# Sums over heads and latents with tokens on the partitions, roots in narrow tiles, spread back by TensorE

## The chip, the cores and the metric

The kernel runs on one core of a Trainium2 chip. The metric is device time in microseconds (us), from the first to the last instruction and what lies around them. Three runs of the kernel before took 2337.64, 2347.23 and 2343.11 us, median 2343.11.

The core has TensorE (matmuls; PE in the profile, its weight loads PEld), VectorE (DVE), ScalarE (ACT), GpSimd (POOL) and SyncE (SP). Matmul results go to PSUM banks of 128 partitions by 512 fp32 values; all else lies in SBUF with 128 partitions.

## The reference, cut to what matters

The model is a decoder trunk of two layers on 512 tokens and 1024 channels. Each layer norms x, projects it, runs four mixers (gated DeltaNet, MLA, RWKV-7, sparse attention), gates and sums their outputs, projects, and adds; then comes an MLP. All of it is fp32. Four places in the mixers divide by a root that belongs to a head and a token, and one divides by a root that belongs to a token:

```python
def rms_norm(x, g, eps=NORM_EPS):
    x32 = x.astype(F32)
    y = x32 * lax.rsqrt(jnp.mean(x32 * x32, axis=-1, keepdims=True) + eps)
    return (y * g.astype(F32)).astype(x.dtype)

def l2_normalize(x, eps=1e-6):
    x32 = x.astype(F32)
    return x32 * lax.rsqrt(jnp.sum(x32 * x32, axis=-1, keepdims=True) + eps)

# RWKV-7, 4 heads of 64
kk = l2_normalize(heads(k * k_k.astype(F32)))                    # the "keys"
o = ((o - mean) * lax.rsqrt(var + RWKV_GN_EPS)).reshape(b, s, RWKV_W) * ln_w + ln_b   # output norm
# gated DeltaNet, 4 heads of 64
q = l2_normalize(q.reshape(b, s, GDN_HEADS, GDN_DK))
k = l2_normalize(k.reshape(b, s, GDN_HEADS, GDN_DK))
o = rms_norm(o, norm_g) * jax.nn.silu(z)                         # gated output norm
# MLA, latents of 256 and 128 channels
q = rms_norm(c_q, q_norm_g) @ w_uq
kv = rms_norm(c_kv, kv_norm_g) @ w_ukv
```

## The kernel before, in words

Activations lie with channels on the partitions and the 512 tokens along the free side. A tile of 128 channels holds two heads of 64, one on partitions 0 to 63 and one on 64 to 127.

**The projections.** The weights come in units of 128 output channels. For each unit ScalarE splits off a high part (L1020), GpSimd makes the low part (L412), and TensorE does 24 matmuls of 512 columns (L451, L452, L455) into one bank. A "gate unit" is such a projection for one tile of a branch's gate. `gates` does two of them, `merge_outputs` (L499) then projects the branch's output `yo` for the two tiles, and VectorE multiplies by the sigmoid and adds (L1390 or L1394). `merge` is both.

**A sum over a head.** `block_sums` multiplies a tile of squares by the constant `blocks`, 128x128 with ones where row and column belong to the same head. So every one of 64 partitions gets the head's sum for 512 tokens: the sum comes out already spread, 128x512 per tile. VectorE adds the epsilon while copying the bank to SBUF, takes the reciprocal of the wide tile, ScalarE takes the root of the wide tile, and VectorE multiplies. For the latents the same is done with the constant `ones` (L849, L853). The sums of the outputs for the mean (L1562) and of r, k and r_k for the bonus (L1524) are block sums too, which the change leaves alone.

**The order.** There is no scheduler. Each engine has its own program in one fixed order, and semaphores join them. Banks go round in three pools: `bank_a` (three banks, read by ScalarE), `bank_v` (four, read by VectorE) and `bank_f` (one). The pool's next bank is used only when its last reader is done. The five places in TensorE's order:

- Keys of RWKV: `block_sums` between two of the eight RWKV projections. VectorE takes the reciprocal (L1502) before mixing tile 5, ScalarE the root (L1100) after copying tile 5.
- Output norm of RWKV and q, k of the delta rule: `block_sums` for both stand behind each other, after the last delta projections, then four gate units, then the wait for `r_out` (VectorE's L1588), then four L499 products. VectorE takes three reciprocals around there (L1576, L1592, L1621), the last behind the gate arithmetic (L1605 widens the gates, L1619 masks the decays). From L1605 TensorE makes the cumulated gates (L771, L775, L557). L1633 makes the last operand of the chunks, which TensorE wants at L532 (transposes).
- Gated output norm: `block_sums` before the second projection of the sparse attention. VectorE's L1651 and ScalarE's L1188 follow.
- Latents of MLA: L849 and L853, then two gate units and two L499 products, then the wait for VectorE's scaled latents (L1756), then the projections of L860.

Further lines that the text names: L545 and L546 (pair matrices of chunks), L1332 (their masks), L532 and L663 (transposes), L612, L632 and L636 (the scan over chunks, in halves of 64 rows), L655 and L673 (attention), L1533 and L1542 (decayed keys and the convolution on VectorE), L1685 (first step of the selection of keys).

Of the kernel before, what the change touches and what calls it, by code (L numbers as in the profile page):

```python
# [22 lines left out]
P = 128  # L23
# [4 lines left out]
TT = T // P  # L28
C = 64
# [47 lines left out]


# [78 lines left out]
def build(nc, x_in, pos_in, wstream, par_in, const_in, tabs, x_dram, out):  # L157
    ctx = ExitStack()
    with ctx:
# [26 lines left out]
        att = sb("att", [P, 3, 4])  # L186

# [56 lines left out]
        for name, n in (  # L244
# [4 lines left out]
            ("r_ex", 1), ("r_sq", 1), ("r_l2", 2), ("r_l2r", 1), ("r_l2s", 1), ("r_bsq", 2), ("r_bon", 2), ("r_feat", 4),  # L249
            ("r_tok", 8), ("r_mat", 8), ("r_x1", 2), ("r_ti", 2), ("r_y", 10), ("r_t", 8), ("r_x", 10),  # L250
            ("r_wt", 2), ("r_y1", 2), ("r_u", 2), ("r_ws", NC), ("r_s", NC), ("r_o", NC),
            ("r_mean", 2), ("r_sq2", 1), ("r_gv", 2), ("r_gr", 1), ("r_gs", 1), ("r_out", 1),
            ("g_in", 6), ("g_z", 2), ("g_conv", 6), ("g_sig", 6), ("g_sq", 1), ("g_l2", 4),
            ("g_l2r", 1), ("g_l2s", 1), ("g_qk", 1), ("g_t1", 1), ("g_sp", 1), ("g_t2", 1), ("g_g", 2), ("g_feat", 6), ("g_gc", 1),
# [3 lines left out]
            ("g_sq2", 1), ("g_gv", 2), ("g_gr", 1), ("g_gs", 1), ("g_out", 1),  # L258
# [3 lines left out]
            ("m_in", 2), ("m_sq", 1), ("m_nv", 2), ("m_rec", 1), ("m_rs", 1), ("m_c", 1), ("m_q", 4), ("m_k", 4), ("m_v", 2),  # L262
# [169 lines left out]
        def _(pe):  # L432
# [213 lines left out]

            def attention(l, x, q_of, k_of, v, fill):
# [46 lines left out]
            for l in range(L):  # L694
# [101 lines left out]
                for i in range(10):  # L796
# [49 lines left out]
                b, reader, emptied = banks.next("v", "m_nv")  # L846
# [433 lines left out]
        def _(dve):  # L1280
# [159 lines left out]
            for l in range(L):  # L1440
# [144 lines left out]
                for f in range(2):  # L1585
                    ts(R["o"][:, f, :], R["o"][:, f, :], pr("ln_w", f), pr("ln_b", f), MUL, ADD)
# [317 lines left out]
```

## Time and profile before

| | before |
|---|---|
| median of 3 runs | 2343.11 us |
| the profiled execution | 2340.02 us |
| its span, first to last instruction | 2338.2 us |
| TensorE busy, share of the span | 2164.7 us, 93% |
| VectorE | 1193.5 us, 51% |
| ScalarE | 722.6 us, 31% |
| GpSimd | 735.5 us, 31% |
| mean granted clock of TensorE, 1 is full | 0.963 |

A busy engine has an instruction under way. [...] "L451" is line 451 of the kernel. Where a wait of TensorE is put down to a line of VectorE, that line's instruction was the last that it waited for. A granted clock of 1.00 is 2.4 GHz and 0.50 is 1.2 GHz.

### The profile page before, as it was taken

What the parts mean: (1) busy time and instruction counts of PE and PEld (TensorE: products, weight loads), DVE (VectorE), ACT (ScalarE), POOL (GpSimd) and SP (SyncE); (2) the same over time, 40 slices, a digit from 0 to 9 for tenths busy, and PEclk for the clock granted to TensorE, in tenths of its full rate; (3) what the DMA queues carried; (4) which work ended last, traced back from release to release, by engine and by line L of the source; (5) the groups of instructions that cost most, each with busy time, mean ns of one, the idle gap of its engine ahead of it and who ended that gap; (6) DMA issues with size and microseconds to landing.
All of it is one profiled execution on the core that took longest, in us unless ns stands there. A gap on an engine that the chain in (4) does not pass through costs nothing.

```text
span 2338.2 us, 34564 instructions
## 1 busy us (share of the span) xinstructions
PE 2164.7 (93%) x14516; PEld 1662.2 (71%) x14516; DVE 1193.5 (51%) x1847; ACT 722.6 (31%) x1102; POOL 735.5 (31%) x550
## 2 busy tenths in 40 slices
PE   6988898998999899999989888799899998999997
PEld 4777686765566688888758766777565676888885
DVE  5885765897473321212168675569956523212212
ACT  3421321233342342323233124023243423322322
POOL 1520211321213344444425022033212242444442
PEclk7999998999999899999989999999999998999998
DMA  4310101221211232323322011012112121233231
GB/s 155 108 62 14 55 29 37 81 77 45 94 51 59 72 106 92 99 91 98 94 95 85 24 43 51 21 57 76 60 50 104 34 90 60 94 99 93 96 99 55
DMA packets 52265, 170.02 MB, mean 73 GB/s; under 512 B 5648, under 2 KB 13968, under 8 KB 51600
## 3 DMA queue, kind: packets, MB, share of 16 engines
q1 hardware_dynamic: 50928, 162.75, 21.8%
q0 software_dynamic: 1184, 5.07, 0.6%
q8 instruction: 116, 1.90, 0.4%
q14 instruction: 37, 0.30, 0.0%
HBM read 160.45 MB, written 7.34 MB: 72 GB/s over the span
## 4 chain that ended last, share of the span: by engine, by line
PE 76%; DVE 20%; ACT 2%; issue 2%; DMA 1%; SPq 0%; DVEq 0%; ACTq 0%
PE bank_a L451 11%; PE bank_a L452 11%; PE bank_a L455 11%; PE bank_v L455 6%; PE bank_v L451 6%; PE bank_v L452 6%; PE bank_v L557 5%; PE bank_v L499 3%; DVE arena L1697 2%; DVE m L1695 2%; DVE arena L1296 2%; PE bank_v L673 2%; PE bank_v L471 2%; DVE s_z L1373 1%; PE bank_v L655 1%
## 5 line engine op out<-in xcount | busy, mean ns | idle before, releaser
L412 POOL TENSOR_TENSOR w_lo<-ring,w_hi 128x512 fp32r<-128x512 f32 x536 | 729.1, 1382 | 1427.5 <-ACT w_hi L1020 1427.4
L451 PE MATMUL bank_a<-h_hi,w_hi 128*128 128x512 f32 x1440 | 591.4, 411 | 31.8 <-DVE h_lo L1320 29.0
L452 PE MATMUL bank_a<-h_lo,w_hi 128*128 128x512 f32 x1440 | 569.0, 395 | 0.0
L1020 ACT ACTIVATE w_hi<-ring 128x1024 fp32r<-128x1024 f32 x268 | 282.1, 1053 | 354.2 <-DVE arena L1806 273.1
L451 PEld LDWEIGHTS bank_a<-h_hi,w_hi 128*128 128x128 f32 x1440 | 274.0, 190 | 122.7 <-issue 45.1
L455 PE MATMUL bank_a<-h_hi,w_lo 128*128 128x512 f32 x1440 | 358.1, 391 | 0.0
L452 PEld LDWEIGHTS bank_a<-h_lo,w_hi 128*128 128x128 f32 x1440 | 275.3, 191 | 62.9 <-issue 9.1
L455 PEld LDWEIGHTS bank_a<-h_hi,w_lo 128*128 128x128 f32 x1440 | 272.1, 189 | 57.6 <-POOL w_lo L412 0.6
L451 PE MATMUL bank_v<-parts,w_hi 128*128 128x512 f32 x640 | 254.4, 398 | 1.4 <-DVE parts L1783 1.4
L452 PE MATMUL bank_v<-parts,w_hi 128*128 128x512 f32 x640 | 253.4, 396 | 0.0
L1806 DVE TENSOR_TENSOR arena<-arena,bank_v 128x512 f32<-128x512 f32 x64 | 44.1, 689 | 306.2 <-PE bank_v L455 306.2
L1797 DVE TENSOR_TENSOR arena<-arena 128x512 f32<-128x512 f32 x64 | 44.3, 692 | 263.6 <-ACT arena L1261 263.6
L455 PE MATMUL bank_v<-parts,w_lo 128*128 128x512 f32 x640 | 162.2, 395 | 0.0
L451 PEld LDWEIGHTS bank_v<-parts,w_hi 128*128 128x128 f32 x640 | 120.3, 188 | 32.7 <-DVE parts L1783 4.0
L452 PEld LDWEIGHTS bank_v<-parts,w_hi 128*128 128x128 f32 x640 | 120.1, 188 | 29.5 <-issue 0.5
L455 PEld LDWEIGHTS bank_v<-parts,w_lo 128*128 128x128 f32 x640 | 120.2, 188 | 29.1
L557 PE MATMUL bank_v<-arena 64*64 64x64 f32 x3712 | 113.6, 221 | 3.8 <-DVE arena L1345 3.8
L557 PEld LDWEIGHTS bank_v<-arena 64*64 64x64 f32 x3712 | 112.7, 137 | 4.5 <-DVE arena L1345 4.2
L499 PE MATMUL bank_v<-yo,out_ring 128*128 128x512 f32 x256 | 114.0, 592 | 0.0
L1296 DVE TENSOR_TENSOR arena<-arena 128x512 f32<-128x512 f32 (+5 forms) x80 | 96.0, 1200 | 18.1 <-ACT arena L1074 15.5
L1261 ACT ACTIVATE arena<-bank_a 128x512 f32<-128x512 f32 x64 | 38.3, 598 | 210.3 <-PE bank_a L455 210.3
L990 ACT ACTIVATE sg<-bank_a 128x512 f32<-128x512 f32 x56 | 33.4, 596 | 217.9 <-PE bank_a L455 108.9
(270 smaller groups left out, 2469.4 us busy)
## 6 DMA issues: line engine op xcount, KB each, us to landing
ring<-in_w SPq DMA_DIRECT2D x268, 512.0 KB, 3.5
out_ring<-in_w SPq DMA_DIRECT2D x64, 128.0 KB, 3.5
x_dram<-arena SPq DMA_DIRECT2D x2, 2048.0 KB, 8.9
arena<-x_dram SPq DMA_DIRECT2D x2, 2048.0 KB, 7.9
arena<-in_x SPq DMA_DIRECT2D x2, 1024.0 KB, 8.4
arena<-tabs POOLq DMA_DIRECT2D x4, 512.0 KB, 3.9
out_x<-arena SPq DMA_DIRECT2D x2, 1024.0 KB, 4.4
par<-in_par POOLq DMA_DIRECT2D x2, 937.0 KB, 7.0
```

The lines of the kernel that those rows point to most:

```text
L412: ins = nc.gpsimd.tensor_tensor(w_lo[:, g % SPLIT, ks, :], raw, w_hi[:, g % SPLIT, ks, :].bitcast(F32), ALU.subtract)
L451: mm(b[:], w_hi[:, s, k, :], hi[:, k, :], start=k == 0, stop=False)
L452: mm(b[:], w_hi[:, s, k, :], lo[:, k, :], start=False, stop=False)
L455: ins = mm(b[:], w_lo[:, s, k, :], hi[:, k, :], start=False, stop=k == KT - 1)
L471: ins = mm(b[:], cst("ones"), squares[n % 2][:, k, :], start=k == 0, stop=k == KT - 1)
L499: ins = mm(b[:], out_ring[:, n % OUT_RING, k, :], yo[:, slot, k, :], start=k == 0, stop=k == 1)
L557: ins = mm(b[quarter(p_), k * C:(k + 1) * C], lhs[quarter(p_), m, :], rhs(m, p_), start=True, stop=True)
L673: ins = mm(b[rows, 0:P], v[:, k, h * C:(h + 1) * C], V_pt(x)[:, j % 2, k, :], start=k == 0, stop=k == qt)
L1020: act_fn(w_hi[:, g % SPLIT, :, :], ring[:, g % RING, :, :], ACT.Copy).then_inc(S["split_hi"], 1)
L1296: link(v.tensor_tensor(out_, a, b, op))
L1695: link(v.max(m8[:], src))
L1697: link(v.match_replace(wk, m8[:], src, -3e38))
```

## The change

The sums are made with tokens on the partitions. `head_sums` takes the tile of squares as the weights, 128 tokens at a time, and moves two columns (one for each head). So a tile of 128 channels by 512 tokens gives 8 columns in one bank; all tiles of a call go into that bank. `head_recip` reads 16 or 32 columns, scales, adds the epsilon and takes the reciprocal, in a small tile `roots`. `head_sqrt` takes the root of the same columns on ScalarE. `spread_roots` takes one column, repeated 64 times, as the weights and moves the identity: that gives a head's root on 64 partitions for 128 tokens. VectorE then reads that bank as an operand of the product, which it used to read from SBUF. For the latents the sums move one column of ones, and the spread has 128 repeated columns.

In TensorE's order the spreads stand: for the keys after one more RWKV projection; for RWKV's output norm between the two pairs of gate units; for q and k after the cumulated gates (L557); for the gated norm after the next projection; for the latents between the gate units and the L499 products, with a wait for VectorE's three products behind these.

```diff
+        roots = sb("roots", [P, 5, 32])
...
+            def head_sums(l, need, k, src, tiles):
+                pe.wait_ge(S[need], at(l, need, k))
+                b, reader, emptied = banks.next("v", "h_sum")
+                pe.wait_ge(reader, emptied)
+                heads = cst("blocks").rearrange("p (x c) -> p x c", c=C)[:, :, 0]
+                for i in range(tiles):
+                    for t in range(TT):
+                        at_ = (i * TT + t) * 2
+                        ins = mm(b[:, at_:at_ + 2], src[:, i, t * P:(t + 1) * P], heads, start=True, stop=True)
+                ins.then_inc(v_full, 1)
+
+            def spread_roots(l, step, tiles):
+                pe.wait_ge(S["h_rt"], at(l, "h_rt", step + 1))
+                for i in range(tiles):
+                    b, reader, emptied = banks.next("v", "h_bc")
+                    pe.wait_ge(reader, emptied)
+                    for t in range(TT):
+                        at_ = (i * TT + t) * 2
+                        for hp in range(2):
+                            ins = mm(b[quarter(hp), t * P:(t + 1) * P], roots[:, step, at_ + hp:at_ + hp + 1].to_broadcast([P, C]),
+                                     cst("ident"), start=True, stop=True)
+                    ins.then_inc(v_full, 1)
...
-                block_sums(l, "r_sq", 1, R["tmp"], 2, "r_l2")
+                head_sums(l, "r_sq", 1, R["tmp"], 2)
                 pe.wait_ge(S["r_act"], at(l, "r_act", 2))
                 low_rank(pr("g2"), R["rm"][:, 7, :])
-                project_rw(3)
+                project_rw(1)
+                spread_roots(l, ROOT_KK, 2)
+                project_rw(2)
...
-                block_sums(l, "r_sq2", 1, R["sq"], 2, "r_gv")
-                block_sums(l, "g_sq", 1, G["sq"], 4, "g_l2")
+                head_sums(l, "r_sq2", 1, R["sq"], 2)
+                head_sums(l, "g_sq", 1, G["sq"], 4)
                 numbers = gates(l, 2, 0)
+                spread_roots(l, ROOT_R, 2)
                 more = gates(l, 2, 1)
                 pe.wait_ge(S["r_out"], at(l, "r_out", 1))
...
                 for half in range(2):
                     chunk_products("v", "g_row", half, ...)
+                spread_roots(l, ROOT_QK, 4)
                 merge(l, 2, 0, 2)
...
                     if i == 1:
-                        block_sums(l, "g_sq2", 1, G["sq2"], 2, "g_gv")
+                        head_sums(l, "g_sq2", 1, G["sq2"], 2)
                     feat_group(("ds", i), l, h_hi, h_lo, "a", "d_in" if i < 8 else "d_vf")
+                    if i == 1:
+                        spread_roots(l, ROOT_G, 2)
...
-                for k in range(2):
-                    ins = mm(b[:], cst("ones"), Mv["sq"][:, k, :], start=k == 0, stop=k == 1)
+                one = cst("ones")[:, 0:1]
+                for t in range(TT):
+                    tokens = slice(t * P, (t + 1) * P)
+                    mm(b[:, t:t + 1], Mv["sq"][:, 0, tokens], one, start=True, stop=False)
+                    mm(b[:, t:t + 1], Mv["sq"][:, 1, tokens], one, start=False, stop=True)
+                for t in range(TT):
+                    tokens = slice(t * P, (t + 1) * P)
+                    ins = mm(b[:, TT + t:TT + t + 1], Mv["sq"][:, 2, tokens], one, start=True, stop=True)
                 ins.then_inc(v_full, 1)
-                mm(b[:], cst("ones"), Mv["sq"][:, 2, :], start=True, stop=True).then_inc(v_full, 1)
-                merge(l, 3, 0, 2)
-                pe.wait_ge(S["m_c"], at(l, "m_c", 1))
+                numbers = gates(l, 3, 2)
+                pe.wait_ge(S["h_rt"], at(l, "h_rt", ROOT_M + 1))
+                for i in range(2):
+                    b, reader, emptied = banks.next("v", "h_bc")
+                    pe.wait_ge(reader, emptied)
+                    for t in range(TT):
+                        ins = mm(b[:, t * P:(t + 1) * P], roots[:, ROOT_M, i * TT + t:i * TT + t + 1].to_broadcast([P, P]),
+                                 cst("ident"), start=True, stop=True)
+                    ins.then_inc(v_full, 1)
+                merge_outputs(0, numbers)
+                pe.wait_ge(S["h_bc"], at(l, "h_bc", 12))
...
+            def head_sqrt(l, step, n):
+                act.wait_ge(S["h_rec"], at(l, "h_rec", step + 1))
+                act_fn(roots[:, step, 0:n], roots[:, step, 0:n], ACT.Sqrt).then_inc(S["h_rt"], 1)
...
-                act_fn(R["tmp"], R["tmp"], ACT.Sqrt).then_inc(S["r_l2s"], 1)
-                act_fn(R["sq"], R["sq"], ACT.Sqrt).then_inc(S["r_gs"], 1)
+                head_sqrt(l, ROOT_R, 16)
+                head_sqrt(l, ROOT_QK, 32)
-                act_fn(G["rs"], G["rs"], ACT.Sqrt).then_inc(S["g_l2s"], 1)
...
+            def head_recip(step, n, scale, eps):
+                dve.wait_ge(v_full, filled.next())
+                b = filled.bank()
+                v.tensor_scalar(roots[:, step, 0:n], b[:, 0:n], scale, eps, MUL, ADD).then_inc(S["h_sum"], 1)
+                dve.wait_ge(S["h_sum"], reached("h_sum"))
+                v.reciprocal(roots[:, step, 0:n], roots[:, step, 0:n]).then_inc(S["h_rec"], 1)
...
-                    v.tensor_scalar(R["tmp"][:, f, :], b[:], EPS, None, ADD).then_inc(S["r_l2"], 1)
-                v.reciprocal(R["tmp"], R["tmp"]).then_inc(S["r_l2r"], 1)
-                tt(R["kk"], R["kk"], R["tmp"], MUL)
+                    v.tensor_tensor(R["kk"][:, f, :], R["kk"][:, f, :], b[:], MUL).then_inc(S["h_bc"], 1)
...
-                v.reciprocal(R["sq"], R["sq"]).then_inc(S["r_gr"], 1)
-                link(v.reciprocal(G["rs"][:, 2:4, :], G["rs"][:, 2:4, :]))
-                v.reciprocal(G["rs"][:, 0:2, :], G["rs"][:, 0:2, :]).then_inc(S["g_l2r"], 1)
+                head_recip(ROOT_R, 16, 1.0 / C, GN_EPS)
+                head_recip(ROOT_QK, 32, 1.0, EPS)
+                    v.tensor_tensor(R["o"][:, f, :], R["o"][:, f, :], b[:], MUL).then_inc(S["h_bc"], 1)
...
+                for i in range(4):
+                    v.scalar_tensor_tensor(G["co"][:, i, :], G["co"][:, i, :], C ** -0.5 if i < 2 else 1.0, b[:], MUL, MUL).then_inc(S["h_bc"], 1)
...
-                v.reciprocal(G["sq2"], G["sq2"]).then_inc(S["g_gr"], 1)
-                stt(G["o"], G["o"], pr("gdn_g", 0), G["sq2"], MUL, MUL)
+                    v.scalar_tensor_tensor(G["o"][:, f, :], G["o"][:, f, :], pr("gdn_g", 0), b[:], MUL, MUL).then_inc(S["h_bc"], 1)
...
-                v.reciprocal(Mv["rs"], Mv["rs"]).then_inc(S["m_rec"], 1)
+                v.reciprocal(roots[:, ROOT_M, 0:2 * TT], roots[:, ROOT_M, 0:2 * TT]).then_inc(S["h_rec"], 1)
```

## Rows read from the trace of the kernel before

**Rows 1.** The page: busy time of each engine; shares of the last chain.

```profile
PE 2164.7 (93%) x14516; PEld 1662.2 (71%) x14516; DVE 1193.5 (51%) x1847; ACT 722.6 (31%) x1102; POOL 735.5 (31%) x550
...
PE 76%; DVE 20%; ACT 2%; issue 2%; DMA 1%; SPq 0%; DVEq 0%; ACTq 0%
```

**Rows 2.** TensorE's waits: us in total, times, longest us.

```profile
PE bank_a L771 <- DVE arena L1605: 12.7, 2, 6.5
...
PE bank_v L655 <- DVE mg L1394: 8.6, 4, 3.4
...
PE bank_v L545 <- DVE arena L1332: 5.7, 2, 2.9
...
PE bank_v L645 <- DVE arena L1569: 4.1, 2, 2.1
```

**Rows 3.** VectorE by line: busy us, mean ns, idle before.

```profile
L1502 DVE RECIPROCAL arena<-arena 128x1024 f32<-128x1024 f32 x2 | 13.1, 6553 | 0.1
```

**Rows 4.** VectorE in order of time: start, us; in brackets idle before.

```profile
113.75 0.69 DVE L1524 TENSOR_TENSOR arena<-bank_v,arena 128x512 f32<-128x512 f32 x1 [7.02 <-PE bank_v L645]
...
263.68 0.69 DVE L1390 TENSOR_TENSOR mg<-bank_v,sg 128x512 f32<-128x512 f32 x1 [2.07 <-PE bank_v L499]
...
283.20 0.17 DVE L1612 COPY gsm<-bank_v 128x16 f32<-128x16 f32 x1 [6.72 <-PE bank_v L775]
...
306.49 2.20 DVE L1633 TENSOR_TENSOR arena<-arena 128x1024 f32<-128x1024 f32 x1
...
432.44 1.12 DVE L1685 TENSOR_SCALAR arena<-arena,ab 128x256 f32<-128x256 f32 x1 [3.11 <-ACT arena L1181]
...
622.34 0.75 DVE L1756 SCALAR_TENSOR_TENSOR misc<-misc,par,arena 128x512 f32<-128x512 f32 x1
```

**Rows 5.** The chain around the changed places: start, us, what.

```profile
112.79 1.73 PE bank_v L645 x4
...
236.38 3.70 PE bank_v L645 x8
...
261.87 6.88 PE bank_v L499 x16
...
275.27 7.69 PE bank_a L771 x48
...
314.21 2.82 PE bank_a L532 x24
```

**Rows 6.** Weight loads by line: busy us, mean ns, idle before.

```profile
L673 PEld LDWEIGHTS bank_v<-arena 128*64 128x64 f32 x320 | 33.5, 138 | 12.6 <-issue 11.9 <-DVE yo L1426 0.7
...
L532 PEld LDWEIGHTS bank_a<-consts,arena 128*128 128x128 f32 x112 | 12.1, 140 | 7.4 <-ACT arena L957 2.9 <-ACT arena L960 2.4 <-issue 1.1
...
L645 PEld LDWEIGHTS bank_v<-arena,consts 128*128 128x128 f32 x56 | 10.4, 189 | 14.2 <-issue 7.2 <-DVE arena L1569 5.8 <-DVE arena L1574 0.5
```

**Rows 7.** Weight loads in order of time; in brackets idle before.

```profile
282.69 0.30 PEld L775 LDWEIGHTS bank_v<-gsm,consts 128*128 128x128 f32 x2
...
591.54 0.19 PEld L451 LDWEIGHTS bank_a<-h_hi,w_hi 128*128 128x128 f32 x1 [0.17 <-issue]
```

**Rows 8.** Small matmuls in order of time: start, us from first start to last end.

```profile
219.06 0.45 PE L632 MATMUL bank_v<-un_z,arena 128*64 128x64 f32 x8
...
283.02 2.08 PE L557 MATMUL bank_v<-consts,gsm 64*64 64x64 f32 x64
...
282.02 0.94 PE L771 MATMUL bank_a<-consts,arena 128*128 128x128 f32 x7
...
589.71 1.91 PE L673 MATMUL bank_v<-arena 128*64 128x128 f32 x16
```

**Rows 9.** Stretches: length, busy us of PE, PEld, DVE, ACT, POOL; granted clock; DMA.

```profile
198.00:201.00 3.00, 1.91 (x51) 1.75 (x48) 1.54 (x5) 0.28 (x1) 0.00 (x0) 1.00 0.00 0
...
274.00:276.00 2.00, 0.73 (x3) 0.73 (x4) 1.93 (x3) 0.23 (x1) 0.00 (x0) 0.50 0.02 8
...
372.00:374.00 2.00, 1.23 (x18) 0.94 (x16) 1.09 (x5) 0.28 (x1) 0.00 (x0) 0.50 0.00 0
```

More of the change, by code:

```diff
@@ L76 @@
 NU = len(UNITS)
+ROOT_KK, ROOT_R, ROOT_QK, ROOT_G, ROOT_M = range(5)
 GATE_STEPS = tuple(range(1, 13))
@@ L1496, in _ @@
                 mix(4)
+                head_recip(ROOT_KK, 16, 1.0, EPS)
+                mix(5)
                 for f in range(2):
@@ L1499, in _ @@
                     b = filled.bank()
[L1500 to L1506 removed]
+                    v.tensor_tensor(R["kk"][:, f, :], R["kk"][:, f, :], b[:], MUL).then_inc(S["h_bc"], 1)
+                    dve.wait_ge(S["h_bc"], reached("h_bc"))
                 dve.wait_ge(S["r_lora"], at(l, "r_lora", 4))
@@ L1573, in _ @@
                     b = filled.bank()
-                    v.tensor_scalar(R["sq"][:, f, :], b[:], 1.0 / C, GN_EPS, MUL, ADD).then_inc(S["r_gv"], 1)
-                    dve.wait_ge(S["r_gv"], reached("r_gv"))
-                v.reciprocal(R["sq"], R["sq"]).then_inc(S["r_gr"], 1)
-                dve.wait_ge(S["r_gr"], reached("r_gr"))
-                for i in range(4):
-                    dve.wait_ge(v_full, filled.next())
-                    b = filled.bank()
-                    v.tensor_scalar(G["rs"][:, i, :], b[:], EPS, None, ADD).then_inc(S["g_l2"], 1)
-                    dve.wait_ge(S["g_l2"], reached("g_l2"))
-                dve.wait_ge(S["r_gs"], at(l, "r_gs", 1))
-                tt(R["o"], R["o"], R["sq"], MUL)
-                for f in range(2):
+                    v.tensor_tensor(R["o"][:, f, :], R["o"][:, f, :], b[:], MUL).then_inc(S["h_bc"], 1)
+                    dve.wait_ge(S["h_bc"], reached("h_bc"))
                     ts(R["o"][:, f, :], R["o"][:, f, :], pr("ln_w", f), pr("ln_b", f), MUL, ADD)
@@ L1744, in _ @@
                 b = filled.bank()
-                v.tensor_scalar(Mv["rs"][:, 0, :], b[:], 1.0 / 256, EPS, MUL, ADD).then_inc(S["m_nv"], 1)
-                dve.wait_ge(S["m_nv"], reached("m_nv"))
+                v.tensor_scalar(roots[:, ROOT_M, 0:TT], b[:, 0:TT], 1.0 / 256, EPS, MUL, ADD)
+                v.tensor_scalar(roots[:, ROOT_M, TT:2 * TT], b[:, TT:2 * TT], 1.0 / 128, EPS, MUL, ADD).then_inc(S["h_sum"], 1)
+                dve.wait_ge(S["h_sum"], reached("h_sum"))
+                v.reciprocal(roots[:, ROOT_M, 0:2 * TT], roots[:, ROOT_M, 0:2 * TT]).then_inc(S["h_rec"], 1)
+                dve.wait_ge(S["h_rec"], reached("h_rec"))
                 dve.wait_ge(v_full, filled.next())
                 b = filled.bank()
-                v.tensor_scalar(Mv["rs"][:, 1, :], b[:], 1.0 / 128, EPS, MUL, ADD).then_inc(S["m_nv"], 1)
-                dve.wait_ge(S["m_nv"], reached("m_nv"))
-                v.reciprocal(Mv["rs"], Mv["rs"]).then_inc(S["m_rec"], 1)
-                dve.wait_ge(S["m_rec"], reached("m_rec"))
-                dve.wait_ge(S["m_rs"], at(l, "m_rs", 1))
-                for f in range(2):
-                    stt(Mv["cq"][:, f, :], Mv["cq"][:, f, :], pr("q_g", f), Mv["rs"][:, 0, :], MUL, MUL)
-                v.scalar_tensor_tensor(misc[:, 0, :], misc[:, 0, :], pr("kv_g", 0), Mv["rs"][:, 1, :], MUL, MUL).then_inc(S["m_c"], 1)
-                dve.wait_ge(S["m_c"], reached("m_c"))
+                stt(Mv["cq"][:, 0, :], Mv["cq"][:, 0, :], pr("q_g", 0), b[:], MUL, MUL)
+                v.scalar_tensor_tensor(Mv["cq"][:, 1, :], Mv["cq"][:, 1, :], pr("q_g", 1), b[:], MUL, MUL).then_inc(S["h_bc"], 1)
+                dve.wait_ge(S["h_bc"], reached("h_bc"))
+                dve.wait_ge(v_full, filled.next())
+                b = filled.bank()
+                v.scalar_tensor_tensor(misc[:, 0, :], misc[:, 0, :], pr("kv_g", 0), b[:], MUL, MUL).then_inc(S["h_bc"], 1)
+                dve.wait_ge(S["h_bc"], reached("h_bc"))
                 merge(l)
```

47 lines of the change are left out of this document (17 added, 30 removed).

## The prediction

> **What bounds the kernel now.** I read the busy shares first: TensorE is busy for 93% of the span, VectorE for 51%, and the chain that ended last is 76% TensorE and 20% VectorE [rows 1]. So what VectorE does counts only where TensorE ends a wait on it. The second view is therefore TensorE's waits by releaser [rows 2]. The entries near the changed places are those before the block sums of q and k (L645 for L1569, 4.1 us in two layers), before the widened gates (L771 for L1605, 12.7 us), before the masked pair matrices (L545 for L1332, 5.7 us) and before an attention (L655 for L1394, 8.6 us). No reciprocal and no square root stands as a releaser of TensorE.
>
> The third view is VectorE's work by line and in order of time, which says why. Each of the six reciprocals of 128x1024 in a layer takes 6.55 us [rows 3], but VectorE is idle afterwards until TensorE delivers: 7.02 us before L1524, 2.07 before L1390 [rows 4]. The fourth view is the chain around the changed places [rows 5]: L645 at 236.38 (q and k sums), L499 at 261.87, VectorE's gate arithmetic, L771 at 275.27, L532 at 314.21. The reciprocals are in none of its steps: they end under TensorE's gate projections, which fill the time from 240 to 262 and from 285 to 296.
>
> **What is removed, on VectorE.** Per layer six reciprocals (39.3 us), twelve copies of 128x512 with an epsilon (0.69 us each, as other reads of PSUM in that size [rows 4], 8.3 us) and wide products. Added are ten narrow operations (0.17 us each, as L1612 [rows 4]) and products that read PSUM, at 0.69 each. VectorE becomes some 43 us per layer less busy. I cost this at nothing for the end time, place by place:
> - Keys of RWKV (before mix 5): VectorE reaches L1524 earlier but waits there for TensorE's L645 as before; its idle 7.02 us grows. The conv work that ends before L545 starts from L1524 and so doesn't start earlier.
> - Output norm of RWKV: the product with the roots must be done before L499 at 261.9. TensorE's spread of the two tiles stands two gate units (10.9 us) before that; VectorE then has some 7 us of work (two products, two affine steps, an add, the output product). It is in time by some 4 us. The idle 6.5 us before L771 start from the last L499 and L1390, behind all this, and stay.
> - q and k of the delta rule: the roots are applied by about 290 and not 298. L1633, which makes the last operand, ends at 308.7 now and near 300 then; TensorE wants it at 314.2 [rows 4, 5]. 5.5 us of slack become 14, and nothing is gained.
> - Gated output norm: nothing of TensorE waits for it until the outputs are merged, much later; the scores behind it start VectorE's selection (L1685) after a wait of 3.11 us [rows 4].
> - Latents of MLA: now VectorE ends them at 623.1 (L1756 [rows 4]), beside two gate units and before the end of two L499 products (8 records, 3.4 us [rows 5]). In the change TensorE waits for VectorE's products behind the spread; three of them (2.3 us) lie beside the same 3.4 us. If that cover were short by a microsecond it would cost that.
>
> ScalarE loses wide square roots and one table load per layer; it is 31% busy and not on the path here. Queues of DMA are not touched.
>
> **What is added, on TensorE.** Every new matmul stands in TensorE's order between others that run without a gap, so each microsecond of it lengthens the chain. An fp32 matmul shows as two records.
> - Removed: 10 block sums and 3 latent sums of 128x512. Two take 1.73 us [rows 5], so 13 x 0.86 = 11.2 us per layer.
> - Head and latent sums: 10 tiles x 4 groups of tokens, and 12 for the latents: 52 matmuls, 104 records, which move 1 or 2 columns and load 128x128 data as weights. So the load decides. The two loads of L775 (16 columns moved) began 0.30 - 0.19 = 0.11 us apart [rows 7]; loads of 128 columns last 189 ns against 138 for 64 [rows 6], so 64 columns are worth 0.05 and 128 about 0.105. I take 0.108: 11.2 us, no change. Bounds: 0.058 each, if they load like the transposes (140 ns, 50 less [rows 6]), -5.2 us per layer; 0.19 each, if loads don't overlap at all, +8.6 us.
> - Spreads over heads: 10 tiles x 4 x 2 matmuls, 160 records that move 128 columns onto 64 rows, alternating between the two halves of a bank. Alternating halves run side by side in the scan: 8 records of L632 with 64 columns took 0.45 us in all, each 0.22, so (0.45 - 0.22)/7 = 0.033 apart. On one half, 16 records of L673 with 128 columns took (1.91 - 0.28)/15 = 0.109 [rows 8]. I take 0.06, near twice the 0.033 for twice the columns: 9.6 us per layer. Bounds 0.053 (8.5) and 0.109 (17.4). That the weights are one column repeated costs nothing: 64 records of L557 with a repeated gate value went by in 2.08 us [rows 8].
> - Spread of the latents: 8 matmuls, 16 records of 128 columns at 0.11 (L771 with 7 records in 0.94 us [rows 8]): 1.8 us.
> - Change of tiling: from 128*64 to 128*128 the load queue stood 0.17 us [rows 7]. Four spreads per layer, two changes each, less one that is there already behind L557: 7 x 0.17 = 1.2 us. Bounds 0 and 1.9 (a record's whole 0.27 us each).
> - Clock: in the windows before L771, with TensorE idle since 269, the granted clock was at half (1.2 GHz); in the scan of the delta rule it stood at 0.50 with TensorE busy for 1.23 of 2 us, in RWKV's scan at 1.00 (2.4 GHz) [rows 9]. The new sums between 232.5 and 240 move two columns at a time, with 2 us of idleness among them. A fall there makes the last sums and the first gates slower, as L771's cold start did: 7.69 us for 48 records [rows 5] against 5.3 at 0.11, so 2.4 us. Bounds 0 and 4 us per layer; I take 2, near L771.
>
> The Trainium skill (TensorEngine Tiling, section Instruction Overhead) gives every matmul a floor of about 60 cycles, so that one column costs what 60 do. If that floor were all that a head sum costs, the estimate from the page would be 0.025 to 0.05 us per record, and the total would be 12 us or more below mine. The same page (Key Properties) says that a change of tiling mode drains TensorE; that speaks against spreading in halves of 64, and rows 7 agree with a price of 0.17 us.
>
> **Sum.** Per layer 0 + 9.6 + 1.8 + 1.2 + 2.0 = 14.6 us, two layers 29. The profiled execution took 2340.0 us (span 2338.2 and 1.8 around it): 2369. The median of the runs shown is 3.1 us above that one, which would give 2372. I say 2371, 1.2% slower.
>
> **Rivals.**
> 1. *Serial spreads or loads.* The halves don't run side by side (0.109): +7.8 us per layer, 2371 + 16 = 2387; with dear loads in part 2395 and over. For it: no row has 128 columns on alternating halves. Against: L632.
> 2. *Cheap sums.* The small matmuls go at 0.058 per record and the clock stays up: -5.2 and -2.0 per layer, 2371 - 14 = 2357. For it: the transposes' shorter loads. Against: L775. The skill's floor, above, points the same way as this rival.
> 3. *VectorE gives back what TensorE pays* (not slower). TensorE's waits on VectorE just behind the changed places are shortened by the freed VectorE: L645 2.05, L771 6.35, L545 2.85, L655 4.3 us per layer, 15.5 in all [rows 2]. If all went, 2371 - 31 = 2340, no change; with cheap sums too, 2326. It decides once VectorE's work before those waits doesn't start from TensorE's own output. For it: VectorE is the named releaser in all four. Against: these stretches of VectorE begin with waits for TensorE (L1524, L1390, L1685 [rows 4]), which is late by what it pays.
> 4. *New waits* (the change doesn't do what it says). TensorE now waits for each set of roots. They should be ready some 3 us early at the keys, 13 at the output norm, 4 at the gated norm, 9 at the latents. At the gated norm sums, two narrow steps, a table load and the root lie under one projection of 5.4 us; a miss by 2 us per layer gives 2375, inside the range.
>
> **Chances.** My forecast with its own range (2360 to 2381) 0.50; rival 1 0.18; rival 2 0.14; rival 3 0.12; rival 4 0.06. A change within 0.5% (12 us) is about what a measurement of this kernel can't tell from none. Slower by more are the forecast, rivals 1 and 4 and 0.08 of rival 2: 0.82. Within it fall 0.06 of rival 2 and 0.06 of rival 3: 0.12. Faster is the rest of rival 3: 0.06. The range reaches past rival 2 below and rival 1 above: 2352 to 2393.
>
> **What would show it.** Right: no reciprocal of 128x1024, VectorE busy for some 85 us less, TensorE's waits for L1569, L1605 and L1332 (under their new numbers) within 1 us of now, a spread of two tiles in about 2 us, head sums of two tiles in about 1.75 us. Wrong: these waits shrink by over 5 us in sum; spread records stand under 0.05 or near 0.11 apart, those of the sums near 0.05 or 0.19; the clock stays at 1.00 through the sums and the gates behind them.

## The result, and the profile after

The changed kernel takes 2373.6 us (median of 4 runs, 2371.9 to 2377.1) against 2341.4 us: ratio 1.0137, 95% interval 1.0112 to 1.0162, so 1.4% slower. 2371 had been forecast. (The baseline is the median of four runs; the fourth came after the forecast.) The page of its profile begins:

```profile
span 2370.1 us, 35584 instructions
PE 2194.4 (93%) x15024; PEld 1701.8 (72%) x15024; DVE 1090.7 (46%) x1843; ACT 710.7 (30%) x1100; POOL 727.5 (31%) x550
```

VectorE's busy share went from 51% [rows 1] to 46%, and the span grew by 31.9 us all the same. TensorE's waits of the kernel after (releaser: us in total, times, longest) are those of [rows 2] under new line numbers:

```profile
PE bank_a L802 <- DVE arena L1648: 12.4, 2, 6.2
PE bank_v L683 <- DVE mg L1449: 9.3, 4, 4.0
PE bank_v L548 <- DVE arena L1387: 6.0, 3, 2.9
PE bank_v L659 <- DVE arena L1621: 4.2, 2, 2.1
```

They were 12.7, 8.6, 5.7 and 4.1. No root stands among them. TensorE in order of time, kernel after (start, us, line, out<-in, count, idle before): the sums and the spread of the keys, then the sums for the output norm, those of q and k (L659), the spread for the output norm (L671), the one of q and k and the one of the latents (L897).

```profile
74.34 1.84 PE L659 MATMUL bank_v<-consts,arena 128*128 128x2 f32 x16
83.42 1.97 PE L671 MATMUL bank_v<-consts,roots 128*64 128x128 f32 x32
...
234.20 1.84 PE L659 MATMUL bank_v<-consts,arena 128*128 128x2 f32 x16
238.13 6.99 PE L659 MATMUL bank_v<-consts,arena 128*128 128x2 f32 x32 [2.08 <-DVE arena L1621]
...
258.74 1.97 PE L671 MATMUL bank_v<-consts,roots 128*64 128x128 f32 x32
...
294.16 3.71 PE L671 MATMUL bank_v<-consts,roots 128*64 128x128 f32 x64
...
635.55 1.95 PE L897 MATMUL bank_v<-consts,roots 128*128 128x128 f32 x16
```

Sixteen sum records (eight matmuls, two records each) in 1.84 us are 0.11 each (records overlap a little; the next matmul starts at 76.04, and 1.70 / 16 = 0.106), a spread of two tiles is 1.9 us. One row stands out: the 32 records of the sums of q and k took 6.99 us, 0.22 each; the eight records of the four block sums that they replace took 3.70 [rows 5]. The windows around it say why (us, then busy time of PE, PEld, DVE, ACT, POOL, then the granted clock, DMA share, GB/s). After:

```profile
232.00:238.00 6.00, 4.04 (x27) 3.56 (x25) 5.93 (x3) 3.58 (x5) 2.32 (x2) 0.92 0.33 112
238.00:246.00 8.00, 7.87 (x35) 7.68 (x36) 1.04 (x5) 0.67 (x3) 2.42 (x2) 0.50 0.25 82
246.00:252.00 6.00, 6.00 (x18) 4.71 (x17) 0.00 (x0) 1.35 (x2) 0.00 (x0) 0.61 0.00 0
252.00:260.00 8.00, 8.00 (x55) 6.56 (x55) 0.05 (x1) 2.70 (x4) 2.54 (x2) 1.00 0.17 44
```

and the same place of the kernel before, where the same wait of 2.05 us stands (L645 at 236.38, [rows 2]: 4.1 us in two layers):

```profile
230.00:236.00 6.00, 4.33 (x16) 2.59 (x14) 5.93 (x3) 3.33 (x5) 2.32 (x2) 1.00 0.33 109
236.00:242.00 6.00, 5.62 (x18) 3.33 (x19) 5.90 (x4) 0.54 (x1) 2.68 (x2) 1.00 0.33 108
242.00:248.00 6.00, 6.00 (x28) 4.99 (x27) 5.83 (x6) 3.57 (x4) 0.00 (x0) 1.00 0.02 4
```

After, TensorE is granted half its clock (1.2 of 2.4 GHz) through the sums of q and k, and more than half of the first gate projection behind them (cold, for short); before, it kept the full one (warm). That is 8 x 0.50 + 6 x 0.39 = 6.3 us of full-clock work lost. In layer 1 the clock fell at the same place.

How much later TensorE reaches the same instruction in the changed kernel, taken from the two timelines (the first L499 behind the output norm starts at 261.71 before and as L502 at 271.65 after, 9.94 later), and what each place adds to this delay:

| place | added, layer 0 / layer 1 (us) | forecast |
|---|---|---|
| keys of RWKV: sums and spread | 2.23 / 2.23 | 2.26 |
| output norm, and sums of q and k | 8.19 / 7.10 | 4.26 |
| spread of q and k | 3.63 / 3.61 | 4.01 |
| gated output norm | 2.16 / 2.16 | 2.26 |
| latents | 1.92 / 3.48 | 1.8 |
| these places together | 18.1 / 18.6 | 14.6 |
| all the unchanged code between them | -3.1 / -1.7 | 0 |

The forecast column splits the prediction's terms over the places (1.92 or 3.84 a spread, 0.17 a change of tiling, 2.0 for the clock). The last two rows give the 31.9 us by which the span grew.

The largest single gain of unchanged code, 1.7 us in layer 0 and 1.6 in layer 1, lies in the selection stretch of the sparse attention. There the granted clock dipped in the profile before and did not in the one after (the same instructions, layer 0; before, then after):

```profile
505.00:513.00 8.00, 5.88 (x11) 2.35 (x10) 6.51 (x10) 3.10 (x6) 1.51 (x1) 0.79 0.26 84
```

```profile
518.90:526.90 8.00, 5.88 (x18) 3.08 (x17) 7.65 (x11) 3.59 (x6) 1.52 (x1) 1.00 0.26 82
```

### The profile page after: what moved, and what is told of

It is laid out like the page before. It is cut to its first block, busy times and chain, and to the rows that moved or that the text cites. A ratio compares the mean times of both kernels' runs of the same rounds, so it can differ in the third digit from the quotient of the medians.

```text
span 2370.1 us, 35584 instructions
## 1 busy us (share of the span) xinstructions
PE 2194.4 (93%) x15024; PEld 1701.8 (72%) x15024; DVE 1090.7 (46%) x1843; ACT 710.7 (30%) x1100; POOL 727.5 (31%) x550
## 3 DMA queue, kind: packets, MB, share of 16 engines
q8 instruction: 120, 1.97, 0.4%
## 4 chain that ended last, share of the span: by engine, by line
PE 76%; DVE 20%; ACT 2%; issue 2%; DMA 1%; SPq 0%; DVEq 0%; ACTq 0%
PE bank_a L454 11%; PE bank_a L455 11%; PE bank_a L458 11%; PE bank_v L458 6%; PE bank_v L454 6%; PE bank_v L455 6%; PE bank_v L560 5%; PE bank_v L502 3%; DVE arena L1736 2%; DVE m L1734 2%; DVE arena L1342 2%; PE bank_v L701 2%; PE bank_v L474 2%; DVE s_z L1428 1%; PE bank_v L683 1%
## 5 line engine op out<-in xcount | busy, mean ns | idle before, releaser
L415 POOL TENSOR_TENSOR w_lo<-ring,w_hi 128x512 fp32r<-128x512 f32 x536 | 721.0, 1367 | 1459.5 <-ACT w_hi L1066 1459.4
L454 PE MATMUL bank_a<-h_hi,w_hi 128*128 128x512 f32 x1440 | 594.8, 413 | 32.2 <-DVE h_lo L1366 29.1
L454 PEld LDWEIGHTS bank_a<-h_hi,w_hi 128*128 128x128 f32 x1440 | 276.6, 192 | 123.7 <-issue 44.9
L458 PE MATMUL bank_a<-h_hi,w_lo 128*128 128x512 f32 x1440 | 358.6, 391 | 0.0
L458 PEld LDWEIGHTS bank_a<-h_hi,w_lo 128*128 128x128 f32 x1440 | 272.8, 189 | 57.4
L454 PE MATMUL bank_v<-parts,w_hi 128*128 128x512 f32 x640 | 254.6, 398 | 1.3 <-DVE parts L1823 1.3
L458 PE MATMUL bank_v<-parts,w_lo 128*128 128x512 f32 x640 | 162.4, 395 | 0.0
L454 PEld LDWEIGHTS bank_v<-parts,w_hi 128*128 128x128 f32 x640 | 120.1, 188 | 33.1 <-DVE parts L1823 4.0
L458 PEld LDWEIGHTS bank_v<-parts,w_lo 128*128 128x128 f32 x640 | 120.1, 188 | 29.2
L502 PE MATMUL bank_v<-yo,out_ring 128*128 128x512 f32 x256 | 114.0, 592 | 0.0
L1342 DVE TENSOR_TENSOR arena<-arena 128x512 f32<-128x512 f32 (+5 forms) x76 | 81.5, 1072 | 33.1 <-ACT arena L1125 30.8
```

The source lines that it names most:

```text
L415: ins = nc.gpsimd.tensor_tensor(w_lo[:, g % SPLIT, ks, :], raw, w_hi[:, g % SPLIT, ks, :].bitcast(F32), ALU.subtract)
L454: mm(b[:], w_hi[:, s, k, :], hi[:, k, :], start=k == 0, stop=False)
L458: ins = mm(b[:], w_lo[:, s, k, :], hi[:, k, :], start=False, stop=k == KT - 1)
L502: ins = mm(b[:], out_ring[:, n % OUT_RING, k, :], yo[:, slot, k, :], start=k == 0, stop=k == 1)
L1342: link(v.tensor_tensor(out_, a, b, op))
```

## The experiments

Ratios are to the kernel before, timed on the same chip; the changed kernel stands at 1.0137, so 0.0010 is 2.3 us. A profile is one execution, and the granted clock differs from one to the next: the four runs of e14 took 2365.6 to 2370.7 us at a mean clock of 0.966 to 0.959, and the profiled one is the slowest of them.

**Is the slow place the wait, or the narrow matmuls?** e1 puts the sums of q and k behind the two gate units, and ScalarE's root between its two merges.

```
-                head_sums(l, "g_sq", 1, G["sq"], 4)
                 numbers = gates(l, 2, 0)
+                head_sums(l, "g_sq", 1, G["sq"], 4)
                 spread_roots(l, ROOT_R, 2)
```

> The changed kernel with one move: the 32 head sums of the queries and keys are issued behind the gates' four merges of the first half (by then their squares are ready), and ScalarE takes their root between its two merges. Theory (the added time beside the spreads is a clock that falls where TensorE waits 2.08 us for the squares and then does 32 two-column sums at 0.50): the wait goes and the sums cost 3.5 instead of 6.99 us, and what follows runs at the full clock: 7 to 8 us a layer, some 15 us in all, so 2358. Rival (the sums are slow in themselves, or the clock falls at the same place without the wait): only the wait goes, 2 us a layer, 2369.

Measured 2360.7, ratio 1.0084 (1.0070 to 1.0099): 13 us less, nearer to the theory. In layer 0 the wait is gone and the sums run warm (at the full clock), but the clock falls a little later, under the spread, which now takes 3.49 instead of 1.97; in layer 1 it falls within the sums (4.48 us) and the spread (3.68). TensorE and windows of this run, layer 0:

```profile
248.98 3.63 PE L659 MATMUL bank_v<-consts,arena 128*128 128x2 f32 x32
252.54 3.49 PE L671 MATMUL bank_v<-consts,roots 128*64 128x128 f32 x32
```

```profile
246.00:252.00 6.00, 6.00 (x42) 5.46 (x41) 0.00 (x0) 2.80 (x3) 3.10 (x3) 1.00 0.34 110
252.00:260.00 8.00, 8.00 (x55) 7.00 (x55) 5.46 (x8) 0.25 (x2) 1.28 (x2) 0.79 0.21 68
```

TensorE had not been idle for a moment from 226 to 266. So idleness just before is not what brings the clock down here.

e9 leaves the order of the changed kernel and makes the sums of q and k 64 columns wide:

```
-  ins = mm(b[:, at_:at_ + 2], src[:, i, t * P:(t + 1) * P], heads, ...)
+  if tiles == 4: ins = mm(b[:, at_ % 16 * 32:at_ % 16 * 32 + 64], src[...], cst("blocks")[:, 0:C], ...)
```

> The changed kernel with the 32 head sums of the queries and keys made 64 columns wide instead of 2, in the same place behind the same wait (the reciprocal reads other columns of them, so the norms are not the reference's). If it is the few columns that let the clock fall at this wait, the granted clock stays at 1.00, the 32 sums cost the same 0.11 us each or less than 0.22, and the place gives back 5 to 6 us a layer: about 2362. If it is the wait of 2.08 us alone that lets it fall, the clock is 0.50 here too, and the time is that of the changed kernel or more: 2374 to 2380.

Measured 2374.4, ratio 1.0142 (1.0128 to 1.0156): nothing. The 16 records of sums ahead of the wait were still two columns wide, and the window behind it is as slow as before (the clock came back a little sooner, 0.82 from 246 to 252 where the changed kernel had 0.61):

```profile
238.00:246.00 8.00, 7.12 (x33) 7.12 (x34) 1.25 (x3) 1.25 (x2) 3.17 (x2) 0.50 0.25 82
```

Read alone, this speaks for the wait. It did not part the two causes, since it left the narrow sums ahead of the wait as they were.

e11 puts the sums of q and k between the two gate units:

```
+                    if j == 1 and between:
+                        between()          # head_sums(l, "g_sq", 1, G["sq"], 4)
```

> As the run in which the head sums of the queries and keys stand behind the two gate units, but between these two units, so that their 32 narrow matmuls and the 32 of the spread that follows no longer stand back to back. Theory (the granted clock falls behind a run of such narrow matmuls; in that run it was 0.50 for some 3.5 us under the spread, which took 3.49 instead of 1.97 us): the clock stays up, 1.7 us a layer less than the 2360.7 measured there, 2357. Rival (16 or 32 of them anywhere let it fall, or it falls for another reason): 2361 or more.

Measured 2362.0, ratio 1.0091 (1.0077 to 1.0105): the theory's gain did not come. In layer 0 the narrow sums start warm, slow down as they go (4.74 us for what took 3.63), and leave the clock at half under full 512-column work, with TensorE busy for 5.00 of 5.00 us (first two windows). In layer 1 the same narrow sums, in the same order, took 3.63 us and the clock did not fall (third window):

```profile
244.34 4.74 PE L661 MATMUL bank_v<-consts,arena 128*128 128x2 f32 x32
```

```profile
243.00:247.00 4.00, 4.00 (x30) 3.77 (x29) 0.00 (x0) 1.54 (x2) 1.17 (x2) 0.95 0.56 164
247.00:252.00 5.00, 5.00 (x17) 4.40 (x18) 0.54 (x2) 0.00 (x0) 1.64 (x2) 0.50 0.42 128
...
1400.00:1404.00 4.00, 4.00 (x31) 3.69 (x29) 0.00 (x0) 1.81 (x3) 1.18 (x2) 1.00 0.54 164
```

e12 is e11, and e14 the changed kernel, with every head sum 128 columns wide. The columns of the blocks are taken in the order head 0, head 1, head 0, ..., and each matmul overwrites the surplus of the one before, so the results stay:

```
-  heads = cst("blocks").rearrange("p (x c) -> p x c", c=C)[:, :, 0]
+  heads = cst("blocks").rearrange("p (x c) -> p c x", c=C)
-  ins = mm(b[:, at_:at_ + 2], ...)
+  ins = mm(b[:, at_:at_ + P], ...)
```

> The changed kernel with every head sum 128 columns wide instead of 2: the two wanted columns come first, the other 126 repeat them and are overwritten by the next matmul, which starts two columns on; order, waits and results are as in the changed kernel. Theory (a stretch of two-column matmuls lets the granted clock fall, also where TensorE is never idle): the clock at the sums of the queries and keys stays near 1.00, as it did in the kernel before with the same wait in the same place; some 6 us a layer less for 32 to 48 sums that now cost 0.12 and not 0.11: 2363. Rival (the wait of 2.08 us, or the number of matmuls, lets it fall): 2374 or more.

Measured 2368.3, ratio 1.0108 (1.0094 to 1.0122). Place, order and wait are the changed kernel's. In layer 0 the clock stays:

```profile
236.10 2.35 PE L659 MATMUL bank_v<-consts,arena 128*128 128x128 f32 x16
240.03 4.63 PE L659 MATMUL bank_v<-consts,arena 128*128 128x128 f32 x32 [1.58 <-DVE arena L1621]
```

```profile
238.00:243.00 5.00, 3.42 (x25) 3.17 (x24) 2.41 (x3) 2.39 (x3) 4.35 (x2) 1.00 0.00 1
243.00:247.00 4.00, 4.00 (x24) 3.58 (x23) 0.55 (x2) 1.51 (x2) 0.00 (x0) 1.00 0.53 164
247.00:252.00 5.00, 5.00 (x23) 4.13 (x22) 0.00 (x0) 1.55 (x2) 0.21 (x1) 1.00 0.00 0
```

In layer 1 it dips all the same, for less long than in the changed kernel; the 32 records took 5.86 us there:

```profile
1400.00:1404.00 4.00, 4.00 (x23) 4.00 (x23) 0.00 (x0) 0.00 (x0) 0.74 (x1) 0.60 0.52 158
```

Sixty-four times the columns, and the time falls by 5.3 us (the four runs of either kernel don't overlap). It isn't the 10 expected: a sum record costs 0.145 and not 0.12, so three groups of 16 pay 0.5 each per layer, and in layer 1 part of the fall was still there.

> The run with the sums between the two gate units (2362.0, granted clock 0.50 in the five us behind them), with every head sum 128 columns wide. Theory: no fall behind the sums, 3 us a layer less, 2356. Rival (the fall has nothing to do with the columns): 2362 or more.

Measured 2364.3, ratio 1.0091 (1.0077 to 1.0104). The clock behaves as the theory has it, 1.00 behind the sums in both layers, where e11 had 0.50 in layer 0 with the same order; the time doesn't follow. Layer 0:

```profile
243.00:247.00 4.00, 4.00 (x26) 3.69 (x25) 0.00 (x0) 1.54 (x2) 0.82 (x2) 1.00 0.53 164
247.00:252.00 5.00, 5.00 (x30) 4.50 (x29) 0.54 (x2) 0.00 (x0) 1.99 (x2) 1.00 0.35 110
```

At 253 us TensorE is 2.0 us ahead of e11. But in layer 1 e11's clock had not fallen, so there was nothing to win, and the dearer sums (0.5 for each group of 16 records, 0.9 for the one of 32) cost 2.4 there, and 0.5 more behind 253 in layer 0. That leaves about nothing, as measured: the spans end 0.3 us apart. The expectation had counted a fall in both layers.

All traces together, each with two layers, for the clock from the start of these 32 records to 8 us behind them. With narrow sums ahead of and behind the wait (changed kernel, e2, e3, e4, e10; e9 with 64 columns behind it) it fell in 12 of 12 places, for 7 to 13 us. With narrow sums and no wait (e1, e11) it fell in 3 of 4, for 3 to 7 us. With 128 columns or 512 behind the wait (e14, kernel before) it fell in 1 of 4, for 3 us; with 128 columns and no wait (e12, e15) in none of 4. So the narrow sums and the wait each go with more and longer falls; what decides the single case isn't shown.

**Does VectorE's saved time count?** e4 puts six wasted reciprocals per layer back, each eight times 128 elements:

```
+        junk = sb("junk", [P, P])
                 dve.wait_ge(S["h_sum"], reached("h_sum"))
+                if step != ROOT_QK: [link(v.reciprocal(junk[:], junk[:])) for _ in range(8)]
                 v.reciprocal(roots[:, step, 0:n], roots[:, step, 0:n])
```

and likewise behind `r_out`, ahead of the products of q and k, and ahead of the latents' reciprocal.

> The changed kernel with wasted reciprocals on VectorE, 1024 elements a partition at each of six places of a layer where the kernel before had its wide ones (eight of 128, one behind the other, some 7 us at a place, 42 us a layer), the sums and spreads left as they are. My theory (VectorE's saved time is off the path to the end): within 5 us of the changed kernel, 2374 to 2379. Rival (VectorE gives back part of what TensorE pays): 10 us a layer or more slower, 2394 or more.

Measured 2393.7, ratio 1.0226 (1.0212 to 1.0240): 20 us slower, which my theory had excluded. All of it arises at two spreads in each layer, where TensorE now waits for the roots (first row: the spread of the keys; second: that of the gated norm, in order of time; then the waits). Both also run cold, 3.4 to 3.5 us instead of 1.97; 13.8 us of waiting and four times 1.5 are the 20:

```profile
87.58 3.50 PE L672 MATMUL bank_v<-consts,roots 128*64 128x128 f32 x32 [3.74 <-ACT roots L1106]
...
418.89 3.40 PE L672 MATMUL bank_v<-consts,roots 128*64 128x128 f32 x32 [3.18 <-ACT roots L1106]
```

```profile
PE bank_v L672 <- ACT roots L1106: 13.8, 4, 3.7
```

In the kernel before, TensorE waited for no wide reciprocal; in e4 it waits for the narrow ones behind the waste. So e10 puts the same waste behind the narrow reciprocals:

```
                 head_recip(ROOT_KK, 16, 1.0, EPS)
+                [link(v.reciprocal(junk[:], junk[:])) for _ in range(8)]
```

> The changed kernel with the same wasted reciprocals on VectorE (six places of a layer, some 7 us each), now put behind the narrow reciprocals and not ahead of them, so that the spreads' inputs are not late. What the run before with the waste ahead of the roots showed (20 us slower, all of it at the first and the last head spread of a layer) is read as two new waits, in which TensorE hangs on the chain of narrow arithmetic. By that theory the waste behind the roots costs next to nothing: 2374 to 2380. Rival (VectorE's saved time itself is on the path): still 15 us a kernel or more, 2389 or later.

Measured 2375.7, ratio 1.0138 (1.0123 to 1.0154): the changed kernel's own. VectorE, kernel e10, in order of time, with 7.87 us of waste at the first place, and the spread not late:

```profile
82.05 7.87 DVE L1555 RECIPROCAL junk<-junk 128x128 f32<-128x128 f32 x8
```

```profile
86.41 1.97 PE L672 MATMUL bank_v<-consts,roots 128*64 128x128 f32 x32
```

VectorE is 93 us busier than in the changed kernel (1183.8 against 1090.7), for nothing.

**What does a spread cost, and the change of tiling?**

```
-  for t in range(TT):  ...  for hp in range(2):      (halves alternate)
+  for hp in range(2):  ...  for t in range(TT):      (e2: halves in turn)
```

> The changed kernel with the loop over the two halves outermost in the spreads: the same 160 matmuls of a layer, but four with the left half of the columns follow one another, then four with the right. If two of them cost 0.12 only because they run side by side in the two halves of the array, each now costs some 0.11: 160 x 0.05 = 8 us a layer more, 2390. If 0.06 is the price of a weight load of 64 columns, whatever its half, nothing changes: 2374.

Measured 2381.5, ratio 1.0171 (1.0157 to 1.0185): 8 us more, half of what the theory gave (ten spreads of two tiles at 0.6 more are 6 of them). TensorE and its weight loads for one spread of two tiles, kernel e2 (1.97 and 1.73 when alternating):

```profile
87.13 2.56 PE L671 MATMUL bank_v<-consts,roots 128*64 128x128 f32 x32
```

```profile
87.13 2.32 PEld L671 LDWEIGHTS bank_v<-consts,roots 128*64 128x64 f32 x32 [0.35 <-issue]
```

So alternation is worth something, 0.08 against 0.06 a record, but the halves in turn are not as slow as the 0.109 of the attention's L673.

e3 makes each spread one matmul over both halves:

```
-  mm(b[quarter(hp), t * P:(t + 1) * P], roots[:, step, at_ + hp:at_ + hp + 1].to_broadcast([P, C]), ...)
+  mm(b[:, t * P:(t + 1) * P], roots[:, step, at_:at_ + 1].to_broadcast([P, P]), ...)
```

> The changed kernel with each spread made as one 128 by 128 matmul instead of two 128 by 64 ones side by side (it spreads the first head's value over both heads of a tile, so the norms are not the reference's): half the instructions, no change of tiling. Theory (a pair of records of 0.06 costs what one full one does, 0.12, and the changes of tiling cost 0.35 in and 0.17 out, five and four times a layer): 2 to 3 us a layer less, 2368. Rival (the side-by-side halves are not really paid for together, or a change of tiling empties more than the load queue): 5 us a layer or more, 2363 or less. Rival (the changes of tiling are hidden): 2374.

Measured 2374.1, ratio 1.0143 (1.0129 to 1.0157): no gain. Kernel e3, the spread of the keys and the gate matmul behind it:

```profile
84.50 1.98 PE L458 MATMUL bank_a<-h_hi,w_lo 128*128 128x512 f32 x8
86.31 1.95 PE L670 MATMUL bank_v<-consts,roots 128*128 128x128 f32 x16
88.01 0.48 PE L454 MATMUL bank_a<-h_hi,w_hi 128*128 128x512 f32 x1
```

From L458 to the next L454 are 3.51 us against 3.80 in the changed kernel (81.51 to 85.31): 0.3 per spread of two tiles with its two changes of tiling. Ten of them are 3 us, less than the 4 to 5 us over which the four runs of either kernel spread, so the time can't show it.

**Order instead of arithmetic.** e8 leaves the kernel before its wide arithmetic, and moves only: sums of q and k behind the two gate units; softplus and the widened gates ahead of the first merges; the keys' reciprocal behind them.

```
-                block_sums(l, "g_sq", 1, G["sq"], 4, "g_l2")
                 numbers = gates(l, 2, 0)
+                block_sums(l, "g_sq", 1, G["sq"], 4, "g_l2")
...
                 dve.wait_ge(S["r_out"], reached("r_out"))
+                (the copies into g_wide and b_wide, then the four copies of the sums)
                 merge(l, True)
                 merge(l, True)
+                link(v.reciprocal(G["rs"][:, 2:4, :], G["rs"][:, 2:4, :]))
```

> The kernel before (wide sums, wide reciprocals), with its order changed alone: the sums of the queries' and keys' squares stand behind the two gate units, the gate arithmetic of the delta branch (softplus, the widened gates) is done before the first merges instead of behind them, and the reciprocal of the keys' half behind these merges. Theory: the wait of 2.05 us for the squares and the wait of 6.2 us for the widened gates go, and with it the 2.3 us that TensorE then loses at a granted clock of 0.61 in six us: 10 us a layer, 2320. Rival (another wait takes their place: the reciprocal of the keys' half now comes late, or TensorE stops for the first merges' outputs): 2330 or more.

Measured 2333.4, ratio 0.9966 (0.9954 to 0.9979). The two waits are gone, but 8 us came of the 20 expected. Part of the rest is lost to other waits; this one among TensorE's waits of e8 was 1.9 us before:

```profile
PE bank_a L451 <- ACT w_hi L1020: 8.7, 7, 2.3
```

ScalarE, in order of time, shows what it hangs on: the root waits for VectorE's wide reciprocal, and the sigmoids, which free the weight buffers, stand behind it.

```profile
247.08 1.06 ACT L1147 ACTIVATE arena<-arena 128x1024 f32<-128x1024 f32 x1 [5.12 <-DVE arena L1582]
248.15 1.28 ACT L990 ACT_TABLE_LOAD   x1
249.45 0.60 ACT L990 ACTIVATE sg<-bank_a 128x512 f32<-128x512 f32 x1
```

e16 swaps the root and the first sigmoid:

```
+                merge_sig(l)
                 act.wait_ge(S["r_gr"], at(l, "r_gr", 1))
                 act_fn(R["sq"], R["sq"], ACT.Sqrt).then_inc(S["r_gs"], 1)
-                merge_sig(l)
                 merge_sig(l)
```

> The kernel before in its changed order (2333.4), with one more move: ScalarE does the two sigmoids of the first gate units, and frees their weight buffers, ahead of the square root for which it waits on VectorE's wide reciprocal. There TensorE waited 2.3 us for these buffers. Theory: that wait and the dip of the clock behind it (0.86) go, 2.5 to 3.5 us a layer: 2328. Rival (something else is late there): 2333.

Measured 2326.2, ratio 0.9927 (0.9914 to 0.9941), the fastest of all. L771, which took 7.69 us cold [rows 5] behind a wait of 6.5 [rows 2], in this run:

```profile
268.39 5.52 PE L771 MATMUL bank_a<-consts,arena 128*128 128x128 f32 x48
```

One wait on wide arithmetic is left. ScalarE's root of q and k waits for VectorE's wide reciprocal (L1621), and the sigmoids that free the weight buffers stand behind it, so TensorE stands for 1.12 and 0.63 us in each layer, 3.5 in all:

```profile
286.92 1.91 ACT L1163 ACTIVATE arena<-arena 128x2048 f32<-128x2048 f32 x1 [4.65 <-DVE arena L1621]
```

e15 gives the changed kernel the same order (sums of q and k behind the gate units, gate arithmetic first), and e14's wide sums.

> The changed kernel with all that the runs point to: gate arithmetic ahead of the first merges (removes the wait of 6.2 us a layer for the widened gates), the sums of the queries and keys behind the two gate units (removes 2.08), head sums 128 columns wide (keeps the clock). From the changed kernel's 2373.6: two layers of 6.2 + 2.1 and some 8 at the clock, 2341. Since its reciprocals are narrow, no wait should take the place of those removed. Rival (as in the reordered kernel before, half of it comes back as other waits): 2355.

Measured 2346.6, ratio 1.0017 (1.0008 to 1.0025): 27 us less than the changed kernel. TensorE isn't idle from 232 to 300, at a clock of 1.00 throughout:

```profile
266.00:272.00 6.00, 6.00 (x15) 2.66 (x14) 2.08 (x3) 3.59 (x5) 0.69 (x1) 1.00 0.08 22
272.00:278.00 6.00, 6.00 (x52) 5.67 (x50) 2.09 (x2) 4.87 (x7) 5.26 (x4) 1.00 0.32 111
```

Beside e16, which has nearly the same order with the wide arithmetic, it is 20.4 us slower, although e16 still has the 3.5 us of waiting. So TensorE pays about 24 us for the spreads and the dearer sums; the forecast has 12.6 a layer for the spreads and changes of tiling alone.

## Why the prediction was right

The time and the mechanism came out as put: TensorE has no slack here, so its added matmuls lengthen the chain, and VectorE's saved time is worth nothing in this order. That the number came out within 3 us is partly luck: the changed places cost 36.7 us and not 29, and unchanged code gave back 4.8. By its steps:

- *VectorE at nothing.* Shown by e10, and by the four waits, unchanged to 0.7 us. VectorE became 103 us less busy, against the 85 forecast. Rival 3 falls with it. e16 shows that this hangs on the order: there the wide reciprocal of q and k does hold TensorE, for 3.5 us. e4 shows the other condition: the saved time has a use only ahead of the roots, because the change put TensorE's spreads behind that chain.
- *Sums at 0.108 a record.* 0.11 measured at the full clock; rival 2's 0.058 falls. The floor of about 60 cycles that the Trainium skill gives (TensorEngine Tiling, Instruction Overhead) was not the price of these matmuls.
- *Spreads at 0.06.* 1.97 us for 32, as forecast. Rival 1 has some truth: out of alternation they cost 0.08, by e2, and not 0.109.
- *Changes of tiling, 1.2 us a layer.* The load queue of the changed kernel stood 0.35 us on the way in and 0.17 on the way out of the keys' spread:

```profile
83.42 1.73 PEld L671 LDWEIGHTS bank_v<-consts,roots 128*64 128x64 f32 x32 [0.35 <-issue]
85.31 0.19 PEld L454 LDWEIGHTS bank_a<-h_hi,w_hi 128*128 128x128 f32 x1 [0.17 <-issue]
```

  But e3, without any, gained nothing that shows. The Trainium skill says that a change of tiling mode drains TensorE (TensorEngine Tiling, Key Properties); by e3 the changes are worth about 0.3 us a spread of two tiles here, both ways and half the records included.
- *Clock, 2.0 us a layer (bounds 0 and 4).* The mis-sized term: 6.3 us in layer 0 by the windows, and the place as a whole exceeds its other terms by 5.9 and 4.8 us, outside the bounds. I had taken a cold start like L771's, a fall behind idleness. e1 and e11 show the clock falling on a busy engine during and behind the two-column sums, and e14 in layer 0 that it can stay up with 128 columns behind the same wait; e11 and e14 in layer 1 show that neither is certain.
- *What made up for it.* Not the other terms: keys, gated norm and spread of q and k came within 0.4 us of theirs. It was the unchanged code. Its largest part is the dip of the clock in the selection stretch, which the profile before had and the one after had not. Nine of the fourteen traces have it in layer 0, on either side of the change, so this is luck. I have no cause for the rest.
- *Latents, 1.8.* 1.92 in layer 0; 3.48 in layer 1, where the clock averaged 0.79 over the eight microseconds behind their narrow sums (it was 1.00 there in the kernel before). No run undid this one alone, but of the 22 places with these sums in eleven traces only three show such a dip (the other two are e10's), so it is no fixed part of the price. The window, kernel after:

```profile
1782.00:1790.00 8.00, 8.00 (x36) 6.77 (x36) 0.94 (x4) 1.49 (x2) 2.86 (x2) 0.79 0.52 164
```

- *Rival 4, new waits.* None in the changed kernel: the root of the keys was ready at 79.95 + 0.22 and its spread began at 83.42, 3 us later, as forecast.

## What to carry to other kernels

Work that is moved from an engine with slack to the one that bounds the kernel is paid in full, however little arithmetic it is; the gain lay in the waits that stood in the profile, and order alone took it (0.7%). Here a tiny matmul cost what its weight load did (0.11 us a record), so look at that first, and at the granted clock where many of them follow one another; look at it in every layer and in more than one profile before you call a dip caused. When one engine is relieved, look at what its shortened chain newly stands in front of.

## What was not expected of the hardware

- The granted clock fell to 0.50 with TensorE busy for 5.00 of 5.00 us, behind 32 records of two columns (e11, layer 0), and stayed at 1.00 with the same records 128 columns wide (e12 in both layers, e14 in layer 0), even across a wait of 1.58 us. The same kernels also show the opposite: 1.00 with two columns (e11, layer 1) and 0.60 over four microseconds with 128 (e14, layer 1).
- A 128x128 matmul that writes 128 columns in place of 2 costs 0.145 a record against 0.11 (4.63 for 32, 1.84 for 16).
- Records of 64 weight columns that alternate between the halves of the array go by in 0.06 us, on one half in turn in 0.08 (e2), and one of 128 columns takes 0.12 (e3).
